# Two transformer blocks in one kernel: other places for some copies, sums and splits in the first attention

## The chip, the cores and the metric

The kernel runs on one core of one Trainium2 chip. The metric is the device time of one execution in microseconds, the median of several. Five engines work side by side, each through its own list of instructions in order: PE (TensorE, matrix products and transposes), DVE (VectorE), ACT (ScalarE), POOL (GpSimd) and SP (SyncE, which here only issues transfers). They meet at semaphores: an instruction waits until a counter has reached a value. An engine that waits holds up all that stands behind in its own list.

## The reference

256 tokens of 1024 numbers go through two blocks, all in float32. The change touches the first block's attention alone:

```python
def rms_norm(x, g):
    xf = x.astype(jnp.float32)
    y = xf * lax.rsqrt(jnp.mean(xf * xf, axis=-1, keepdims=True) + RMS_EPS)
    return (y * g.astype(jnp.float32)).astype(x.dtype)

# diff_attention: 4 heads, each with two maps of 64; moba_attention: 8 heads of 64 (one block of 256 keys)
q = rms_norm(q, q_g); k = rms_norm(k, k_g)          # per head
logits = where(dist >= 0, einsum(q, k) * scale + bias, NEG_INF)
p = softmax(logits)
w = p[:, :, 0] - lam * p[:, :, 1]                    # differential heads only
out = einsum(w, v)
out = rms_norm(out, sub_g) * (1.0 - lambda_init)     # differential heads, per head of 128
...
# first block: x + concat(diff, moba) @ w_out, then x + hier_moe(rms_norm(x))  (32 experts, 2 per token)
# second block: feed forward, window attention and mLSTM, gates, feed forward, final norm
```

## The kernel before, in words

**Precision.** PE multiplies float32 numbers in a faster mode (`float32r`) that keeps fewer digits, so each operand is split into a high part (rounded) and a low part (the rest), and each product is three: high by high, low weight by high, high weight by low (L1072 to L1074).

**Weights.** All dense weights stream through in pieces of 1 MB (128 x 2048 numbers). SP loads a piece into one of three slots (`load`), ACT writes its high part (`split`, L678, 1.9 us), DVE its low part (`split_at`, L1787, 2.3 us), and PE multiplies with it. `feed(q)` on ACT and on DVE splits all pieces up to q + 2 that are not split yet. ACT's split of piece n waits for its transfer and until PE has used piece n - 2 (`piece_used`); the load of piece n waits for DVE's split of piece n - 3 (`split_lo`).

**First attention.** Pieces 0 to 11 are the input projection, two pieces for each of six projections of 512 columns: q and k of the differential heads (projections 0, 1), q and k of the other heads (2, 3), the values of both (4, 5). Tokens come in two halves ("tiles") of 128, t = 0 and 1. For projections 0 to 3:
- ACT squares the result (`qk_squares`, L734), DVE sums per head (`head_squares_of`, L1849), POOL takes the power -1/2 (`root`, L559) and DVE multiplies (`take_projection`, L1867);
- PE transposes the rows (`qk_transpose`, L1143) and ACT copies them out of PSUM into `qkT`, times the gain (`qk_copy(p, t)`, L724).

PE has the scores between its projection products in six bursts (`first_scores`, L1160); DVE adds the bias and takes the maximum (`first_logits`, L1874, L1892), ACT the exponentials (`first_exps`, L739), DVE weighs the two maps (`differential_weights`). Then come, for t = 0 and t = 1, the transposes of the weights on PE (`first_weights`, L1224), their copies by ACT and DVE in turn (`pT_copy`, L709 and L1813), and the products with the values (`first_values(t, units)`, L1253: units 0 to 3 are the differential heads, 128 columns each, and units 4 to 11 the others, 64 columns each). ACT squares the differential heads' output (`heads_squared`, L783), DVE sums it per head, POOL takes the root, DVE multiplies both kinds of heads into `token_major` (`normed_heads`, L1938 to L1946). PE transposes that (`transpose8_tile`, L1089) and ACT and DVE split it into high and low (`t8_split`, L701, L702, L1806, L1807). Last comes the output projection with pieces 12 to 15 (`w_out_part(column half, piece half, t)`), then the router and the expert stage.

**Order.** Nothing is planned by a program: each engine's list stands as written in its block. Queues that matter here: SP's list loads the pieces in turn, waits for 12 used pieces before the gate and up weights of expert 1, for all four value products (`pv` at 4) before those of expert 0, for 16 split pieces before expert 2, and for 16 used pieces before experts 3 and 4. POOL's list has the roots in the order in which DVE asks for them.

## Time and profile before

| | us |
|---|---|
| median of 3 runs | 1100.5 |
| lowest, highest | 1098.31, 1100.85 |
| the profiled execution's own time | 1099.94 |
| its span in the trace | 1098.2 |
| PE busy in it | 1037.1 (94%) |
| DVE, ACT busy | 555.3, 428.0 |

The profile gives for each engine its busy time and, on a timeline, each instruction's start and length, with the idle time before it and who ended that in brackets (short idle times have no bracket). The chain is followed back from the last instruction. Start times are from the start of the span.

### The profile page before, as it was taken

Reading aid. Unit: us, or ns where it says so; the run is one execution under the profiler, and the core shown is the slowest. Engines: PE = TensorE matmul, PEld = TensorE weight load, DVE = VectorE, ACT = ScalarE, POOL = GpSimd, SP = SyncE. Lnnn points to the kernel's source line nnn. Section 1 sums busy time; section 2 is a strip of 40 time slices with the busy share of each in tenths; the row PEclk is TensorE's granted clock in tenths of the full one; section 3 lists DMA queues with packets and bytes.
Section 4 is the critical chain, followed back from the end, with each engine's and each line's share of the span. In section 5 each row is a group of like instructions: output and inputs, shape, how many; then the busy total and the mean of one; then the engine's idle time right before and its main releaser. Section 6 shows DMA issues by size and latency. Waiting matters only on the chain.

```text
span 1098.2 us, 13293 instructions
## 1 busy us (share of the span) xinstructions
PE 1037.1 (94%) x5337; PEld 793.8 (72%) x5337; DVE 555.3 (51%) x844; ACT 428.0 (39%) x564; POOL 48.5 (4%) x57
## 2 busy tenths in 40 slices
PE   7989889999999999999999999978999999999997
PEld 6877777654444458878788899855888888877875
DVE  5477463122222255444546547497656665444443
ACT  4365232322222144343344444384344344444342
POOL 2330000000000000000000000010100010000000
PEclk9999899999999999999999999888999999999999
DMA  8864385999999957555654555411165637555540
GB/s 287 259 228 153 154 349 196 380 418 420 422 421 421 421 170 257 189 185 165 190 187 153 192 177 188 138 54 39 50 239 190 192 115 229 173 191 159 185 153 38
DMA packets 101820, 239.59 MB, mean 218 GB/s; under 512 B 11666, under 2 KB 56810, under 8 KB 86282
## 3 DMA queue, kind: packets, MB, share of 16 engines
q1 hardware_dynamic: 99850, 229.05, 58.0%
q0 software_dynamic: 1920, 9.85, 2.6%
q8 instruction: 34, 0.56, 0.2%
q14 instruction: 16, 0.13, 0.0%
HBM read 237.81 MB, written 3.43 MB: 220 GB/s over the span
## 4 chain that ended last, share of the span: by engine, by line
PE 77%; DVE 8%; issue 5%; ACT 5%; SPq 2%; DMA 2%; POOL 1%; DVEq 0%; ACTq 0%; POOLq 0%
PE banks L1072 17%; PE banks L1074 16%; PE banks L1073 16%; PE banks L1368 8%; PE banks L1393 5%; ACT weights_hi L678 4%; PE banks L1348 3%; PE banks L1377 3%; DMA raw_weights<-in_w_in 2%; DVE stage L2136 1%; DVE weights_lo L1787 1%; PE banks L1079 1%; PE banks L1089 1%; PE banks L1492 1%; SPq L488 1%
## 5 line engine op out<-in xcount | busy, mean ns | idle before, releaser
L1787 DVE TENSOR_TENSOR weights_lo<-raw_weights,weights_hi 128x2048 fp32r<-128x2048 f32 x116 | 265.7, 2291 | 215.4 <-ACT weights_hi L678 215.2
L678 ACT ACTIVATE weights_hi<-raw_weights 128x2048 fp32r<-128x2048 f32 x116 | 221.7, 1912 | 171.7 <-PE banks L1074 154.1
L1072 PE MATMUL banks<-weights_hi,normed_T_hi 128*128 128x512 f32 (+1 forms) x624 | 248.9, 399 | 9.8 <-DVE stage L2136 7.6
L1074 PE MATMUL banks<-weights_hi,normed_T_lo 128*128 128x512 f32 (+1 forms) x624 | 243.4, 390 | 0.0
L1073 PE MATMUL banks<-weights_lo,normed_T_hi 128*128 128x512 f32 (+1 forms) x624 | 242.6, 389 | 0.0
L1072 PEld LDWEIGHTS banks<-weights_hi,normed_T_hi 128*128 128x128 f32 x624 | 118.4, 190 | 42.0 <-DVE stage L2136 13.3
L1074 PEld LDWEIGHTS banks<-weights_hi,normed_T_lo 128*128 128x128 f32 x624 | 118.0, 189 | 25.2
L1073 PEld LDWEIGHTS banks<-weights_lo,normed_T_hi 128*128 128x128 f32 x624 | 118.4, 190 | 22.6
L1072 PE MATMUL banks<-weights_hi,ffn_hidden_T_hi 128*128 128x512 f32 x160 | 62.4, 390 | 0.0
L1074 PE MATMUL banks<-weights_hi,ffn_hidden_T_lo 128*128 128x512 f32 x160 | 62.3, 389 | 0.0
L1073 PE MATMUL banks<-weights_lo,ffn_hidden_T_hi 128*128 128x512 f32 x160 | 62.2, 389 | 0.0
L2064 DVE TENSOR_TENSOR stage<-stage,banks 128x256 f32<-128x256 f32 x16 | 6.7, 422 | 88.7 <-ACT stage L825 88.7
L1368 PE MATMUL banks<-expert_weights,token_major 128*64 128x512 f32 x160 | 49.5, 594 | 0.0
L2056 DVE SCALAR_TENSOR_TENSOR expert_out_lo<-banks,slot_weights,expert_out_hi 128x512 fp32r<-128x512 f32 x32 | 24.0, 750 | 48.2 <-ACT expert_out_hi L831 48.1
L893 ACT ACTIVATE ffn_hidden_T_hi<-banks 128x512 fp32r<-128x512 f32 x20 | 12.0, 598 | 92.3 <-PE banks L1492 92.3
L831 ACT ACTIVATE expert_out_hi<-banks,slot_weights 128x512 fp32r<-128x512 f32 x32 | 22.0, 688 | 61.6 <-PE banks L1393 61.6
L825 ACT ACTIVATE stage<-banks 128x256 f32<-128x256 f32 x16 | 6.2, 386 | 95.7 <-PE banks L1368 71.7
L2160 DVE TENSOR_TENSOR ffn_hidden_T_lo<-banks,ffn_hidden_T_hi 128x512 fp32r<-128x512 f32 x20 | 13.8, 692 | 58.4 <-ACT ffn_hidden_T_hi L893 58.4
L1079 PE MATMUL banks<-ident 128*128 128x128 f32 x244 | 33.7, 298 | 7.8 <-POOL rel_bias L586 7.3
L559 POOL TENSOR_TENSOR rstd<-rstd,minus_half 128x1 f32<-128x1 f32 x12 | 8.6, 721 | 730.5 <-DVE rstd L1753 730.3
L1074 PE MATMUL banks<-normed_T_hi,weights_lo 128*128 128x256 f32 x144 | 40.8, 283 | 0.0
L1073 PE MATMUL banks<-normed_T_lo,weights_hi 128*128 128x256 f32 x144 | 40.8, 283 | 0.0
(358 smaller groups left out, 1664.6 us busy)
## 6 DMA issues: line engine op xcount, KB each, us to landing
raw_weights<-in_w_in SPq DMA_DIRECT2D x38, 1024.0 KB, 5.0
raw_weights<-in_ffn_w_gate SPq DMA_DIRECT2D x44, 512.0 KB, 3.9
raw_weights<-in_ffn_w_up SPq DMA_DIRECT2D x44, 512.0 KB, 4.9
raw_weights<-in_ffn_w_down SPq DMA_DIRECT2D x22, 1024.0 KB, 4.8
stage<-in_w_down SPq DMA_DIRECT2D x14, 1024.0 KB, 12.1
expert_weights<-in_w_gate SPq DMA_DIRECT2D x12, 1024.0 KB, 11.2
expert_weights<-in_w_up SPq DMA_DIRECT2D x12, 1024.0 KB, 13.2
expert_weights<-in_w_down SPq DMA_DIRECT2D x12, 1024.0 KB, 14.3
```

What stands on the lines that cost most here:

```text
L678: ins = eng.activation(w_hi[:, slot, :], raw, ACT.Copy)
L831: eng.activation(exo[0][:, h * HALF:(h + 1) * HALF], PS[:, 7 - h, :], ACT.Copy, scale=wslot[:, 0:1]).then_inc(ex_hi, 1)
L1072: eng.matmul(dst, x[0], w[0], start=first_one, stop=False)
L1073: eng.matmul(dst, x[0], w[1], start=False, stop=False)
L1074: return eng.matmul(dst, x[1], w[0], start=False, stop=last_one)
L1079: eng.matmul(PS[:, bank, 0:P], ident[:, :], ident[:, :], start=True, stop=True)
L1348: mm = eng.matmul(PS[:, 2 * t + h, :], selT[:, u, t * P:(t + 1) * P], exo[x][:, h * HALF:(h + 1) * HALF], start=(first_one and x == 0), st ...
L1368: mm = eng.matmul(PS[SLOTS * m:SLOTS * (m + 1), 6, :], rows[:, k, at + SLOTS * m:at + SLOTS * (m + 1)], gate_up(s)[:, k], start=(k == 0), ...
L1377: mm = eng.matmul(PS[SLOTS * m:SLOTS * (m + 1), 6, cut], rows[:, k, at + SLOTS * m:at + SLOTS * (m + 1)], gate_up(s)[:, k, side], start=(k ...
L1393: mm = eng.matmul(PS[SLOTS * m:SLOTS * (m + 1), 7 - h, :], hidT_e[:, k, SLOTS * m:SLOTS * (m + 1)], down(s)[:, k, h * HALF:(h + 1) * HALF] ...
L1787: ins = eng.tensor_tensor(w_lo[:, slot, :], raw, w_hi[:, slot, :], ALU.subtract)
L2056: eng.scalar_tensor_tensor(exo[1][:, cut], PS[:, 7 - h, :], wslot[:, 0:1], exo[0][:, cut], ALU.mult, ALU.subtract).then_inc(done, 1)
```

## The change

It moves work within four lists and adds or takes away no operation on data.

- **ACT, k rows.** `qk_copy(1, 0)` and `qk_copy(1, 1)` go from behind the split of piece 8 to ahead of the split of piece 7, right behind `qk_copy(0, ...)`.
- **ACT, output.** The split of piece 13 goes ahead of the last exponentials (`first_exps(4, 1, 1)`), the split of piece 14 and the square of half 0's heads ahead of the copies `pT_copy((0, 1))`, the square of half 1's heads ahead of the split of half 0's transposed output.
- **DVE.** `normed_heads` is cut in two. `head_sums` has the reciprocal, the sum per head and the request to POOL; `normed_heads` waits for the root and multiplies. The sums of half 0 go ahead of `pT_copy((0, 1))`, behind the low part of piece 13; the sums of half 1 ahead of the split of half 0; the low part of piece 14 behind both halves.
- **PE.** The transposes of half 0's output stand behind four units of half 1's value products instead of eight; those of half 1 behind one quarter of the output projection instead of two.

```diff
                 if p == 2:
-                    for t in range(TILES):
-                        qk_copy(0, t)
+                    for n in range(2):
+                        for t in range(TILES):
+                            qk_copy(n, t)
                 feed(2 * p + 1)
...
             feed(6)
-            for t in range(TILES):
-                qk_copy(1, t)
             feed(7)
...
             first_exps(3, 0, 1)
+            feed(11, BEFORE_MOE)
             first_exps(4, 1, 1)
             pT_copy((0, 0))
-            pT_copy((0, 1))
-            feed(11, BEFORE_MOE)
+            feed(12, BEFORE_MOE)
...
             heads_squared(0)
-            feed(12, BEFORE_MOE)
+            pT_copy((0, 1))
+            heads_squared(1)
             t8_split(T_Y, yT, vec[:, V_SUB:V_SUB + 1], (0,))
-            heads_squared(1)
...
-            first_values(1, range(8))
+            first_values(1, range(4))
             transpose8_tile(0, tok, (mixed, 2), False)
-            first_values(1, range(8, 12))
+            first_values(1, range(4, 12))
...
             w_out_part(0, 0, 0)
+            transpose8_tile(1, tok, (mixed, 4), False)
             w_out_part(0, 1, 0)
-            transpose8_tile(1, tok, (mixed, 4), False)
...
-            def normed_heads(t):
+            def head_sums(t):
                 eng.wait_ge(expd, EXP_START[t, 1] + MOBA_HEADS)
                 eng.reciprocal(hs[:, t, 5, 8:16], hs[:, t, 2, 8:16])
                 eng.wait_ge(pv_sq, t + 1)
                 link(eng.tensor_reduce(hs[:, t, 7, 0:4], flat(L[t])[:, 0:HALF].rearrange("p (h c) -> p h c", h=4), AX_X, ALU.add))
-                rsqrt(hs[:, t, 7, 4:8], hs[:, t, 7, 0:4], 2 * HEAD)
+                roots[0] += 1
+                eng.tensor_scalar(hs[:, t, 7, 4:8], hs[:, t, 7, 0:4], 1.0 / (2 * HEAD), EPS, ALU.mult, ALU.add).then_inc(root_in, 1)
+                return roots[0]
+
+            def normed_heads(t, root):
+                eng.wait_ge(root_out, root)
...
             take_projection(5)
+            feed(11, BEFORE_MOE)
+            root = head_sums(0)
             pT_copy((0, 1))
-            feed(11, BEFORE_MOE)
-            normed_heads(0)
+            normed_heads(0, root)
+            root = head_sums(1)
+            t8_split(T_Y, yT, vec[:, V_SUB:V_SUB + 1], (0,))
+            normed_heads(1, root)
             feed(12, BEFORE_MOE)
-            t8_split(T_Y, yT, vec[:, V_SUB:V_SUB + 1], (0,))
-            normed_heads(1)
             t8_split(T_Y, yT, vec[:, V_SUB:V_SUB + 1], (1,))
```

The instruction lists show it at three places. First ACT's list around the k rows, before: `weights_hi` is the high part of a piece (7, 8 and 9 here behind 6), L724 the copies of transposed q or k rows.

```order
L678 ACTIVATE weights_hi<-raw_weights 128x2048
L724 ACTIVATE stage<-banks,vec 128x4x128 x2
L678 ACTIVATE weights_hi<-raw_weights 128x2048
L755 ACTIVATE lambda_parts<-lambda_parts 128x2
L757 ACTIVATE router_hi_lo<-router 128x8x36
L759 ACTIVATE w_if_hi<-w_if 128x128
L734 ACTIVATE token_major<-banks 128x512 x2
L678 ACTIVATE weights_hi<-raw_weights 128x2048
L724 ACTIVATE stage<-banks,vec 128x4x128 x2
L678 ACTIVATE weights_hi<-raw_weights 128x2048
```

and with the change:

```order
L678 ACTIVATE weights_hi<-raw_weights 128x2048
L724 ACTIVATE stage<-banks,vec 128x4x128 x4
L678 ACTIVATE weights_hi<-raw_weights 128x2048
L756 ACTIVATE lambda_parts<-lambda_parts 128x2
L758 ACTIVATE router_hi_lo<-router 128x8x36
L760 ACTIVATE w_if_hi<-w_if 128x128
L734 ACTIVATE token_major<-banks 128x512 x2
L678 ACTIVATE weights_hi<-raw_weights 128x2048 x2
```

Two copies left the place between pieces 8 and 9 and stand between pieces 6 and 7.

Second ACT's list from the exponentials of half 0's second group (L739, 128x128) to the split of half 0's output (L701, L702), before:

```order
L739 ACTIVATE conv_room,head_stats<-conv_room,head_stats 128x128 x8
L739 ACTIVATE stage,head_stats<-stage,head_stats 128x256 x8
L709 ACTIVATE conv_room<-banks 128x512
L709 ACTIVATE stage<-banks 128x512 x3
L678 ACTIVATE weights_hi<-raw_weights 128x2048
L783 ACTIVATE conv_room<-banks 128x512
L678 ACTIVATE weights_hi<-raw_weights 128x2048
L701 ACTIVATE mixed_T_hi<-banks,vec 128x4x128
L702 ACTIVATE mixed_T_hi<-banks 128x4x128
L783 ACTIVATE stage<-banks 128x512
```

and with the change:

```order
L739 ACTIVATE conv_room,head_stats<-conv_room,head_stats 128x128 x8
L678 ACTIVATE weights_hi<-raw_weights 128x2048
L739 ACTIVATE stage,head_stats<-stage,head_stats 128x256 x8
L709 ACTIVATE conv_room<-banks 128x512
L678 ACTIVATE weights_hi<-raw_weights 128x2048
L782 ACTIVATE conv_room<-banks 128x512
L709 ACTIVATE stage<-banks 128x512 x3
L782 ACTIVATE stage<-banks 128x512
L701 ACTIVATE mixed_T_hi<-banks,vec 128x4x128
L702 ACTIVATE mixed_T_hi<-banks 128x4x128
```

Both splits (pieces 13 and 14) and both squares (L782) stand earlier; the three copies of half 1 (L709, `stage`) stand later.

Third DVE's list from the values' copy of projection 5 on, before: L1813 copies transposed weights of half 1, L1940 is the sum per head, L1942 and L1946 the two multiplications into `token_major`.

```order
L1862 COPY stage<-banks 128x512 x2
L1813 COPY stage<-banks 128x512 x3
L1787 TENSOR_TENSOR weights_lo<-raw_weights,weights_hi 128x2048
L1938 RECIPROCAL head_stats<-head_stats 128x8
L1940 TENSOR_REDUCE head_stats<-conv_room 128x4
L1747 TENSOR_SCALAR head_stats<-head_stats 128x4
L1942 TENSOR_TENSOR token_major<-banks,head_stats 128x512
L1946 TENSOR_TENSOR token_major<-banks,head_stats 128x512
L1787 TENSOR_TENSOR weights_lo<-raw_weights,weights_hi 128x2048
L1806 SCALAR_TENSOR_TENSOR mixed_T_lo<-banks,vec,mixed_T_hi 128x4x128
L1807 TENSOR_TENSOR mixed_T_lo<-banks,mixed_T_hi 128x4x128
```

and with the change:

```order
L1861 COPY stage<-banks 128x512 x2
L1786 TENSOR_TENSOR weights_lo<-raw_weights,weights_hi 128x2048
L1937 RECIPROCAL head_stats<-head_stats 128x8
L1939 TENSOR_REDUCE head_stats<-conv_room 128x4
L1941 TENSOR_SCALAR head_stats<-head_stats 128x4
L1812 COPY stage<-banks 128x512 x3
L1946 TENSOR_TENSOR token_major<-banks,head_stats 128x512
L1950 TENSOR_TENSOR token_major<-banks,head_stats 128x512
L1937 RECIPROCAL head_stats<-head_stats 128x8
L1939 TENSOR_REDUCE head_stats<-stage 128x4
L1941 TENSOR_SCALAR head_stats<-head_stats 128x4
L1805 SCALAR_TENSOR_TENSOR mixed_T_lo<-banks,vec,mixed_T_hi 128x4x128
```

The low part of piece 13 and the sums of half 0 went ahead of the three copies, and the low part of piece 14 is gone from between the multiplications and the split of half 0.

## Rows read from the trace of the kernel before

**Rows 1.** The page: the chain that ended last, by engine.

```profile
PE 77%; DVE 8%; issue 5%; ACT 5%; SPq 2%; DMA 2%; POOL 1%; DVEq 0%; ACTq 0%; POOLq 0%
```

**Rows 2.** Waits of PE, 40 to 147 us (total, times, longest us).

```profile
PE banks L1089 <- DVE token_major L1946: 3.7, 1, 3.7
PE banks L1160 <- ACT stage L724: 2.8, 1, 2.8
```

**Rows 3.** Timeline of PE, first scores (start, length, idle before in brackets).

```profile
61.93 1.34 PE L1160 MATMUL banks<-stage 64*128 64x128 f32 x16 [2.76 <-ACT stage L724]
...
70.17 1.03 PE L1143 MATMUL banks<-ident,token_major 128*128 128x128 f32 x8
...
78.93 0.66 PE L1143 MATMUL banks<-ident,token_major 128*128 128x128 f32 x4
```

**Rows 4.** Timeline of ACT, k rows to the first exponentials.

```profile
54.42 1.92 ACT L678 ACTIVATE weights_hi<-raw_weights 128x2048 fp32r<-128x2048 f32 x1 [4.15 <-DMA raw_weights<-in_w_in]
...
61.21 1.25 ACT L724 ACTIVATE stage<-banks,vec 128x512 f32<-128x512 f32 x2
...
67.77 0.40 ACT L739 ACTIVATE conv_room<-conv_room,head_stats 128x128 f32<-128x128 f32 x1 [3.52 <-DVE head_stats L1892]
...
71.83 1.91 ACT L678 ACTIVATE weights_hi<-raw_weights 128x2048 fp32r<-128x2048 f32 x1
```

**Rows 5.** Timeline of DVE in the same stretch.

```profile
67.65 2.28 DVE L1787 TENSOR_TENSOR weights_lo<-raw_weights,weights_hi 128x2048 fp32r<-128x2048 f32 x1
72.32 0.43 DVE L1874 CUSTOM_DVE_ANT_0 stage<-banks,stage 128x256 f32<-128x256 f32 x1 [2.39 <-PE banks L1160]
...
75.29 2.28 DVE L1787 TENSOR_TENSOR weights_lo<-raw_weights,weights_hi 128x2048 fp32r<-128x2048 f32 x1
77.49 0.68 DVE L1867 TENSOR_TENSOR token_major<-banks,head_stats 128x512 f32<-128x512 f32 x1
```

**Rows 6.** Timeline of POOL: two roots of projection 2, one of half 0's heads.

```profile
60.72 4.41 POOL L559 TENSOR_TENSOR head_stats<-head_stats,minus_half 128x8 f32<-128x8 f32 x2 [13.14 <-DVE head_stats L1853]
...
114.02 1.01 POOL L559 TENSOR_TENSOR head_stats<-head_stats,minus_half 128x4 f32<-128x4 f32 x1 [34.95 <-DVE head_stats L1747]
```

**Rows 7.** Timeline of PE, value products of half 1 and the transposes.

```profile
108.93 3.79 PE L1253 MATMUL banks<-stage 128*128 128x128 f32 x32 [0.69 <-ACT stage L709]
116.40 1.97 PE L1089 MATMUL banks<-ident,token_major 128*128 128x128 f32 x8 [3.68 <-DVE token_major L1946]
118.16 3.51 PE L1253 MATMUL banks<-stage 128*128 128x64 f32 x16
```

**Rows 8.** Timeline of ACT, last exponentials and the split of piece 13.

```profile
96.42 0.51 ACT L739 ACTIVATE stage<-stage,head_stats 128x256 f32<-128x256 f32 x1 [4.51 <-DVE head_stats L1892]
...
108.78 1.90 ACT L678 ACTIVATE weights_hi<-raw_weights 128x2048 fp32r<-128x2048 f32 x1
```

**Rows 9.** Timeline of DVE, low part of piece 13 to that of piece 14.

```profile
110.71 2.29 DVE L1787 TENSOR_TENSOR weights_lo<-raw_weights,weights_hi 128x2048 fp32r<-128x2048 f32 x1 [2.17 <-ACT weights_hi L678]
...
115.06 0.69 DVE L1942 TENSOR_TENSOR token_major<-banks,head_stats 128x512 f32<-128x512 f32 x1 [1.19 <-POOL head_stats L559]
...
116.26 2.28 DVE L1787 TENSOR_TENSOR weights_lo<-raw_weights,weights_hi 128x2048 fp32r<-128x2048 f32 x1
```

**Rows 10.** Stretches (length, busy us and instructions of PE, PEld, DVE, ACT, POOL; PEclk, DMA share, GB/s).

```profile
114.00:116.00 2.00, 0.00 (x0) 0.00 (x0) 0.94 (x2) 0.00 (x0) 1.01 (x1) 0.50 0.01 4
...
320.00:350.00 30.00, 28.78 (x134) 12.72 (x132) 7.53 (x16) 6.07 (x10) 0.00 (x0) 1.00 1.01 421
```

**Rows 11.** The chain in order of time: output projection (start, us).

```profile
123.92 0.43 PE banks L1074
124.34 0.24 PE banks L1072
```

**Rows 12.** Timeline of PE, second products of two expert pairs in a row.

```profile
355.20 0.61 PE L1393 MATMUL banks<-expert_weights,stage 128*64 128x512 f32 x1 [0.61 <-DVE stage L2066]
...
369.05 0.61 PE L1393 MATMUL banks<-stage 128*64 128x512 f32 x1 [0.61 <-DVE stage L2066]
```

## The prediction

> **What bounds the kernel now.** First the page: 77% of the chain that ended last is PE [rows 1], so a change on ACT or DVE is worth what it takes from PE's waits and from its stretches at half clock. Second the waits of PE in the first attention: two are long, 3.7 us for half 0's output in `token_major` and 2.8 us for copied k rows [rows 2]; the change aims at both. Third the timelines around each, to see what is late next. Fourth the clock: a long wait is followed by products at half pace.
>
> *The k wait.* PE is through projection 3's first piece at 61.93 - 2.76 = 59.2 and stands until ACT's second k copy is out [rows 3]. ACT was not short of time: it idled 4.15 us before piece 7 for that piece's transfer, but had the k copies behind piece 8 [rows 4].
>
> *The output wait.* PE ends eight units of half 1's values at 112.7 and waits until 116.4 [rows 7]. Behind that wait is a row of single steps: ACT splits piece 13 (108.78, [rows 8]), DVE takes its low part (110.71), sums, has the root from POOL (1.01 us, [rows 6]) and multiplies (115.06, then the second product) [rows 9]. In the wait the clock is at 0.50 [rows 10], 1.2 of 2.4 GHz, and it stays there: eight transposes take 1.97 us where eight took 1.03 [rows 3, 7], 16 products of 64 columns 3.51 us where 32 took 3.79 [rows 7], and the wide products start every 0.43 us until 124.34, then every 0.24 [rows 11].
>
> **Part 1, the k rows.** PE's transposes of k stand 24 products before 59.2; at 0.23 to 0.24 us each [rows 11] they end near 53.7. ACT is idle then. The second copy starts there and takes 1.25/2, so both are out at about 54.4, when piece 7 lands (54.42, [rows 4]). Piece 7 is delayed by 0.1 us at most, and nothing behind it waits.
>
> PE then has the first scores at 59.2 to 60.5, projection 3's second piece to 66.1, the transposes of projection 2 to 67.0. What is late next is DVE: the second burst of scores waits until the first burst's maxima are taken, that is until DVE starts piece 9's low part at 67.65 [rows 5]. Nothing moves DVE up to there (its list waited for projection 2's roots on POOL, 60.72 to 65.13, [rows 6]). So PE waits some 0.7 us, has scores to 68.8, products to 74.4, the third burst to 75.5, and needs projection 3's multiplied rows. On DVE those stand behind piece 10's low part. Its high part is made on ACT behind the first exponentials, which start at 67.77 whatever the change does, so at 71.83 + 1.91 = 73.74 [rows 4] as before. Before, DVE came to it only at 75.29, because the second logits waited for PE until 72.32 [rows 5]. Now DVE ends piece 9 at 69.9 and needs 75.29 - 72.32 = 2.97 us for these logits and the sums: 72.9, before 73.74. So piece 10 starts at 73.8, the multiplication 77.49 - 75.29 = 2.20 us later at 76.0, and it ends at 76.7. PE's transposes stood at 78.93 [rows 3]: **2.2 us** earlier. PE stands about 1.2 us there, shorter than either long wait.
>
> From there to the values the rest keeps its distance: PE, whose products run without a long wait, leads; the roots and exponentials have moved by 1.5 us or more with half a microsecond or more to spare. Bounds of this term: 0 (piece 10 keeps its time after all, should POOL's roots delay DVE) and 4.1 (the 2.76 us and 1.3 us of half pace, nothing late next). I take 2.2, the value the rows give.
>
> **Part 2, the output.** All times below are before's less 2.2. ACT's split of piece 13 goes into the idle 4.51 us before the last exponentials [rows 8]: it needs 11 used pieces, which PE gives 2 to 3 us before those exponentials are due, and takes 1.9: hidden. Were it late, the exponentials would be, and through them the transposes of weights, one for one. The split of piece 14 falls in the time in which ACT only waits for transposes and values of half 0.
>
> DVE: the values' copy ends at 101.4, piece 13's low part takes 2.2 (101.3 to 103.6), reciprocal, sum and request 0.9 to 104.5. The first of the three copies of half 1 is ready at about 104.0, so it is 0.4 us late; PE needs its bank again only when it has transposed four banks, near 105.1: hidden, 0.1 at most. Copies end at 106.4; the root, asked at 104.5, takes 1.01 alone and half of 4.41 beside DVE [rows 6], so by 106.7; both multiplications end at 107.6 to 108.0. PE starts half 1's values at 106.8; four units take 3.79/2 = 1.9, to 108.6. So the transposes find their rows, with 0.6 to 1.0 us to spare, and the 3.68 us wait is gone.
>
> What is late next? The split of half 0: transposes to 109.6, ACT 1.2, DVE 1.3, ready at 112.3. PE covers it with eight units, 3.79 us, to 113.3: 1 us to spare. Half 1: squares at 109.3, its root by 111.5 to 112.7, multiplications behind the last values (113.3) to 114.1; PE is in one quarter of the output projection (12 products, 2.8 us) to 116.0. Its split is ready by 120, used at 122.6. Piece 14's low part ends by 116.6, used near 119.8; piece 15 waits for PE as before.
>
> If PE does not stand, the half clock behind the wait goes too. It cost 1.97 - 1.03 = 0.94 (transposes), 3.51 - 3.79/2 = 1.61 (values), and of the 2.8 us of wide products to 124.34 the share 1 - 0.24/0.43, 1.25. **Sum of part 2:** 3.68 + 0.94 + 1.61 + 1.25 = 7.5 us. Bounds: 0 (another step takes the wait's place whole) and 7.5.
>
> **Behind it.** SP issues expert 1's gate and up 2.2 us earlier, expert 0's weights with `pv` 4 about 8 us earlier, experts 2 to 4 with the end of the output projection, as far before it as ever. The expert stage, POOL's list and the second block keep their distances: 0.
>
> **Total.** 2.2 + 7.5 = 9.7 us. The profiled execution took 1099.94 us (span 1098.2), so 1090.2; it lies 0.56 under the median of the runs, and on the median's footing this is 1100.5 - 9.7 = **1090.8**.
>
> **Rival A: the clock falls without a wait.** Half 1's values with 64 columns now stand in one run of 32 products, not 16 + 16, behind eight transposes. Before, the clock fell after 16 such products and part of the wait [rows 7, 10], and 16 of them at half clock did not bring it back; only the wide products did. Against it: up to 112.7 PE had just had 24 transposes and 16 narrow products and ran 32 at 0.118 us each, full pace [rows 7]. If it falls halfway through the run, 16 products cost 1.61 and the wide ones 1.25 again: 1090.8 + 2.9 = 1093.7. A rule bears on it: the Trainium skill (TensorE: Matmul & The Clock Gate, Part 4: PE-mode transpose) has it that transposes on PE don't count as busy for the clock. By that rule the transposes ahead of the narrow run speak for the fall, and the time would be this rival's; the full pace at 108.93, right behind the weights' transposes, doesn't bear it out.
>
> **Rival B: part 1 gives nothing.** DVE and ACT set the pace between 60 and 80 us, and PE only waits elsewhere (at the second burst and the q rows). For it: POOL's roots took 4.41 us for two [rows 6], and a later one holds DVE. Against: the root of the first half is asked at about 72.2 and has 3.8 us. Then 1100.5 - 7.5 = 1093.0.
>
> **Rival C: slower, by the experts' weights.** From 320 to 350 us the queues are full (share 1.01, 421 GB/s) [rows 10], while PE takes a pair every 369.05 - 355.20 = 13.85 us [rows 12]. A pair's six transfers of 1024 KB are 6.3 MB, 14.9 us at that rate: the weights lose 1.1 us on PE with each pair and live on the lead from the loads before. If the shorter attention ate that lead, PE would go at 14.9 for some 12 pairs, 13 us: 1090.8 + 13 = 1103.8. It decides from the point where the lead is 9.7 us too short. Against it: loads 0 and 2 to 4 hang on counters that move with PE, so the lead moves along, and PE shows no wait for a transfer there.
>
> **Rival D: no change.** Both waits come back in another place (ACT's list is tight, or the half clock stays): 1100 to 1101.
>
> **Chances.** Forecast 0.68 (its own range 1089.2 to 1092.4), A 0.15, B 0.12, C 0.02, D 0.03. The range to 8 in 10 takes in A and B's middle: 1088.8 to 1094.0. About 0.3%, 3.3 us, can be told from no change; forecast, A and B lie beyond it: faster 0.95, same 0.03, slower 0.02.
>
> **What would show it.** In the changed kernel's trace: no idle before PE's first scores and their start near 59.2; a wait of under 1 us before the second burst and of about 1 before projection 3's transposes, those near 76.7; the transposes of half 0 near 108.6 without a wait, clock 1.00 to the end of the output projection; its last product 9.7 us earlier than before; every later stretch as long as before. Wrong would be: exponentials pushed behind piece 13, a wait for `mixed_T_lo` before the first quarter, a clock of 0.50 behind the 64-column run, or waits for weights among the experts.

## The result, and the profile after

| | before | changed |
|---|---|---|
| median of the first comparison, us | 1099.7 (15 runs) | 1092.6 (15 runs) |
| lowest, highest | 1096.7, 1102.3 | 1087.6, 1095.9 |
| the profiled execution's own time | 1099.94 | 1090.14 |
| its span | 1098.2 | 1088.3 |
| PE busy in it | 1037.1 | 1031.6 |

The ratio is 0.9932 [0.9918, 0.9946]: 7.1 us between the medians, 9.8 us between the two profiled executions. The forecast was 9.7 us, as a time 1090.8, and the range 1088.8 to 1094.0 holds the median. Two later comparisons of the same kernels gave 0.992 [0.9895, 0.9945] and 0.991 [0.989, 0.9931]. Over all three the mean of 49 executions of before is 1100.6 and that of 27 of the changed kernel 1092.0: 8.6 us (7.6 to 9.6). So the profiled execution of the changed kernel is 1.9 us better than its mean, that of before 0.6 us; why executions of one kernel differ is a question of its own below.

The chain by engine has nearly kept its shape [rows 1]. PE's share has grown from 77 to 79%, and the 4% of SP's queue and of transfers (SPq, DMA) are no longer in it:

```profile
PE 79%; DVE 8%; issue 6%; ACT 6%; POOL 1%; DVEq 0%; ACTq 0%; POOLq 0%
```

Waits of PE from 40 to 147 us, the stretch of [rows 2]. Both long ones are gone:

```profile
PE banks L1142 <- DVE token_major L1866: 1.2, 1, 1.2
PE banks L1088 <- DVE token_major L1758: 1.0, 1, 1.0
PE banks L1159 <- DVE head_stats L1873: 0.9, 1, 0.9
PE banks L1252 <- ACT conv_room L709: 0.8, 1, 0.8
PE banks L1252 <- ACT stage L709: 0.7, 1, 0.7
PE banks L1312 <- DVE routed_T_lo L1803: 0.6, 1, 0.6
```

The first and the third are new, the two short waits that the prediction named as "what is late next". The second and the sixth stand behind the output projection; before has them too, with 1.0 and 0.6 us, but past 147 us. PE's timeline at the first scores, for [rows 3]: the scores start 2.7 us earlier without a wait, projection 3's transposes 2.1 us earlier (76.86, before 78.93).

```profile
59.24 1.16 PE L1159 MATMUL banks<-stage 64*128 64x128 f32 x16
65.92 1.03 PE L1142 MATMUL banks<-ident,token_major 128*128 128x128 f32 x8
...
67.83 1.14 PE L1159 MATMUL banks<-stage 64*128 64x256 f32 x8 [0.88 <-DVE head_stats L1873]
...
76.86 0.66 PE L1142 MATMUL banks<-ident,token_major 128*128 128x128 f32 x4 [1.17 <-DVE token_major L1866]
```

ACT in the same stretch, for [rows 4]: the k rows stand in the idle time before piece 7, and the split of piece 7 starts 0.16 us later than before.

```profile
53.43 1.27 ACT L724 ACTIVATE stage<-banks,vec 128x512 f32<-128x512 f32 x2 [4.46 <-PE banks L1142]
54.58 1.92 ACT L678 ACTIVATE weights_hi<-raw_weights 128x2048 fp32r<-128x2048 f32 x1
```

DVE, for [rows 5]: piece 10's low part now waits for ACT's high part, not for PE.

```profile
67.80 2.28 DVE L1786 TENSOR_TENSOR weights_lo<-raw_weights,weights_hi 128x2048 fp32r<-128x2048 f32 x1
...
73.92 2.29 DVE L1786 TENSOR_TENSOR weights_lo<-raw_weights,weights_hi 128x2048 fp32r<-128x2048 f32 x1 [0.60 <-ACT weights_hi L678]
76.13 0.68 DVE L1866 TENSOR_TENSOR token_major<-banks,head_stats 128x512 f32<-128x512 f32 x1
```

PE in the output, for [rows 7]. Four units, eight transposes and eight units follow each other without a wait and at full pace:

```profile
106.95 2.05 PE L1252 MATMUL banks<-stage 128*128 128x128 f32 x16 [0.69 <-ACT stage L709]
108.84 1.04 PE L1088 MATMUL banks<-ident,token_major 128*128 128x128 f32 x8
109.72 3.68 PE L1252 MATMUL banks<-stage 128*128 128x64 f32 x32
```

ACT, for [rows 8]: piece 13's split stands in the idle time ahead of the last exponentials, and 0.81 us of it is left.

```profile
91.59 1.91 ACT L678 ACTIVATE weights_hi<-raw_weights 128x2048 fp32r<-128x2048 f32 x1 [1.79 <-PE banks L1073]
94.32 0.51 ACT L739 ACTIVATE stage<-stage,head_stats 128x256 f32<-128x256 f32 x1 [0.81 <-DVE head_stats L1891]
```

DVE, for [rows 9]: low part, sums, three copies, two multiplications. The root comes from POOL beside the copies (for [rows 6]), and the rows are ready at 107.8, 1.0 us before PE's transposes.

```profile
101.38 2.28 DVE L1786 TENSOR_TENSOR weights_lo<-raw_weights,weights_hi 128x2048 fp32r<-128x2048 f32 x1
...
103.69 0.63 DVE L1939 TENSOR_REDUCE head_stats<-conv_room 128x4 f32<-128x512 f32 x1
...
106.48 0.68 DVE L1946 TENSOR_TENSOR token_major<-banks,head_stats 128x512 f32<-128x512 f32 x1
107.08 0.68 DVE L1950 TENSOR_TENSOR token_major<-banks,head_stats 128x512 f32<-128x512 f32 x1
```

```profile
104.67 1.01 POOL L559 TENSOR_TENSOR head_stats<-head_stats,minus_half 128x4 f32<-128x4 f32 x1 [26.97 <-DVE head_stats L1941]
```

Stretches, with the columns of [rows 10]. The clock is 1.00 throughout the output, and the transfers among the experts are as before:

```profile
107.00:110.00 3.00, 3.00 (x28) 3.00 (x28) 1.19 (x4) 0.68 (x2) 0.00 (x0) 1.00 0.00 0
110.00:114.00 4.00, 4.00 (x35) 3.87 (x35) 3.04 (x6) 1.09 (x2) 1.01 (x1) 1.00 0.02 4
...
118.00:136.00 18.00, 18.00 (x81) 14.90 (x80) 5.68 (x7) 3.38 (x4) 0.29 (x1) 1.00 0.71 287
320.00:350.00 30.00, 28.78 (x132) 12.55 (x130) 8.30 (x18) 7.33 (x12) 0.00 (x0) 1.00 1.01 420
```

The last product of the first attention, before and then changed (PE's timeline): it starts 9.7 us earlier, and that is the gain of the pair but for 0.2 us (the spans differ by 9.9).

```profile
145.51 0.39 PE L1074 MATMUL banks<-weights_hi,mixed_T_lo 128*128 128x512 f32 x1
```

```profile
135.80 0.39 PE L1073 MATMUL banks<-weights_hi,mixed_T_lo 128*128 128x512 f32 x1
```

### The profile page after: what moved, and what is told of

Read it like the earlier page. It is cut to its first block, busy times and chain, and to the rows that moved or that the text cites. A ratio compares the mean times of both kernels' runs of the same rounds, so it can differ in the third digit from the quotient of the medians.

```text
span 1088.3 us, 13293 instructions
## 1 busy us (share of the span) xinstructions
PE 1031.6 (95%) x5337; PEld 790.1 (73%) x5337; DVE 555.3 (51%) x844; ACT 428.1 (39%) x564; POOL 49.1 (5%) x57
## 4 chain that ended last, share of the span: by engine, by line
PE 79%; DVE 8%; issue 6%; ACT 6%; POOL 1%; DVEq 0%; ACTq 0%; POOLq 0%
PE banks L1071 17%; PE banks L1073 17%; PE banks L1072 17%; PE banks L1367 8%; PE banks L1392 5%; ACT weights_hi L678 4%; PE banks L1347 3%; PE banks L1376 3%; DVE stage L2142 1%; PE banks L1078 1%; DVE weights_lo L1786 1%; PE banks L1088 1%; PE banks L1491 1%; PE banks L1252 1%; PE banks L1223 1%
```

## The experiments

Each kernel was timed beside the kernel before, whose medians were 1099.7 to 1101.4. This table takes the starts of four groups on PE's timeline from each profile; "A" is from half 1's first value product to the last product of the output, "B" from there to the end of the span.

| kernel | scores | projection 3's transposes | half 1's values | last product | A | B | median, us |
|---|---|---|---|---|---|---|---|
| before | 61.93 | 78.93 | 108.93 | 145.51 | 36.6 | 952.7 | 1099.7 to 1101.4 |
| k rows alone | 59.07 | 77.51 | 107.52 | 144.74 | 37.2 | 953.3 | 1099.4 |
| output alone | 62.70 | 79.70 | 109.83 | 138.63 | 28.8 | 953.4 | 1092.7 |
| changed | 59.24 | 76.86 | 106.95 | 135.80 | 28.9 | 952.5 | 1092.6 |
| changed, second | 59.62 | 77.53 | 107.67 | 136.48 | 28.8 | 952.5 | 1091.0 |
| changed, third | 59.68 | 77.30 | 107.44 | 136.28 | 28.8 | 952.8 | 1091.2 |
| wide values | 59.77 | 77.39 | 107.52 | 136.36 | 28.8 | 952.8 | 1092.6 |
| PE's order old | 59.65 | 77.27 | 107.36 | 137.45 | 30.1 | 954.5 | 1092.7 |
| PE's order new, lists old | 59.58 | 77.20 | 107.21 | 146.68 | 39.5 | 952.5 | 1102.4 |
| more idle products | 59.31 | 76.94 | 107.03 | 135.87 | 28.8 | 952.5 | 1090.6 |
| sums late | 61.55 | 79.55 | 109.56 | 139.52 | 30.0 | 952.5 | 1093.8 |
| split late | 59.84 | 77.57 | 107.58 | 136.39 | 28.8 | 956.1 | 1091.7 |
| narrow products mixed in | 59.34 | 76.97 | 107.06 | 135.86 | 28.8 | 952.3 | 1089.6 |

**Part 1 alone.** The first part of the change, on the kernel before:

```diff
-                    for t in range(TILES):
-                        qk_copy(0, t)
+                    for n in range(2):
+                        for t in range(TILES):
+                            qk_copy(n, t)
...
-            for t in range(TILES):
-                qk_copy(1, t)
```

> Part 1 of the change alone: the two k copies ahead of the split of piece 7, all else as before. Theory (the changed kernel's trace): PE's first scores start near 59.2 without a wait, projection 3's transposes near 76.8 instead of 78.93, and the 3.7 us wait at the output stays, 2.1 us earlier: 2.0 to 2.3 us faster than before in the median, about 1097.5. Rival (part 1 carries no gain, what the first parts save comes back at the waits of 0.9 and 1.2 us with a fallen clock): 0 to 0.5 us.

Measured: 1099.43, ratio 0.9988 [0.9971, 1.0005]. As a time that is 0.5 us slower to 3.2 us faster: neither no change nor the expected 2.0 to 2.3 us is ruled out, and the median is 0.7 us under that of before, not 2. In its trace the k wait is gone, but projection 3's transposes come only 1.4 us earlier and the last product 0.8 us. Piece 7 was not there yet when ACT had done the copies:

```profile
55.23 1.92 ACT L678 ACTIVATE weights_hi<-raw_weights 128x2048 fp32r<-128x2048 f32 x1 [0.70 <-DMA raw_weights<-in_w_in]
```

The output wait stands, as long as before and with the same eight transposes at half pace:

```profile
114.99 1.97 PE L1088 MATMUL banks<-ident,token_major 128*128 128x128 f32 x8 [3.68 <-DVE token_major L1945]
```

In before's profile the wide products are back at full pace from 124.1 us, here from 124.0, though the work came 1.4 us earlier. So nine of them, not six, ran at half pace, and A is 0.6 us longer:

```profile
115.00:120.00 5.00, 5.00 (x24) 5.00 (x25) 3.93 (x5) 1.66 (x3) 0.00 (x0) 0.50 0.00 0
120.00:124.00 4.00, 4.00 (x11) 3.14 (x11) 1.67 (x4) 0.00 (x0) 1.01 (x1) 0.50 0.65 227
124.00:130.00 6.00, 6.00 (x31) 5.06 (x30) 0.18 (x1) 1.18 (x2) 0.00 (x0) 0.98 0.95 365
```

**Part 2 alone.** All other edits, k rows where they were.

> Part 2 alone: the new order of splits, sums, squares and transposes at the output, k copies where they were. Theory: the wait of 3.7 us and the half clock behind it go, 7.5 us in an execution whose clock stays up and about 5 in the median, 1094.5, because in some executions the clock falls in or behind the run of 64-column products. Rival (the median's missing 2.6 us belongs to the k part): the full 7.5 us in the median, 1092.2.

Measured: 1092.65, ratio 0.9911 [0.9882, 0.994]. That is the rival's 1092.2, not the theory's 1094.5. A falls by 7.8 us (36.6 to 28.8), and is the same with the k rows moved too. In this profile and in the second of the changed kernel ACT had piece 6 at the same time (47.96 and 48.04); between them the k rows move the last product from 138.63 to 136.48: 2.15 us. The timed runs of the two don't show it: the medians are 1092.65 and 1091.05, the means of six executions each 1091.6 and 1091.9.

**The changed kernel again,** without an edit.

> The changed kernel once more, for a second profile and the spread of its times. Theory (clock): times spread over some 8 us in two groups by mean granted clock, one near 1090 at 0.984 and one near 1093 to 1095 at 0.978 to 0.981, and a profile out of the second group shows a stretch of 0.50 in the first attention that the first profile does not have, behind the 64-column products. Rival (transfers or waits vary): a slow execution shows a longer wait of PE there at full clock.

Measured: 1091.05, ratio 0.992 [0.9895, 0.9945], the same picture, 0.7 us later from the second burst on (68.50 for 67.83).

**Wider value products.** For rival A: 14 of the 16 narrow products of half 1 take 128 columns in place of 64 (the added columns are overwritten by the next unit). The trace has two rows for each of these products, 32 in all; the prediction and the expectations count rows.

```diff
-                            dst, v = PS[:, 2 * t + 1, h * HEAD:(h + 1) * HEAD], vals[:, kb, HALF + h * HEAD:HALF + (h + 1) * HEAD]
+                            n = 2 * HEAD if t == 1 and u < 11 else HEAD
+                            dst, v = PS[:, 2 * t + 1, h * HEAD:h * HEAD + n], vals[:, kb, HALF + h * HEAD:HALF + h * HEAD + n]
```

> The changed kernel with half 1's value products of the second kind of heads made 128 columns wide instead of 64: the upper 64 columns of each are the next head's place and are written anew by the next head's product, so the output stays. Rows of 64 and of 128 columns took the same 0.118 us, so in an execution without a clock fall nothing changes (1090). Theory (the clock falls because of the narrow run): the group of slower executions goes, median 1090 to 1091, 2 us under the changed kernel. Rival (the clock falls elsewhere, at the waits of 0.9 and 1.2 us or later): same spread and median as the changed kernel, 1092.6.

Measured: 1092.61, ratio 0.9926 [0.9898, 0.9954]. Neither the time nor the pace moves: the products take 3.68 us at 64 columns and at 128. Its row of PE's timeline, then its stretch:

```profile
110.28 3.68 PE L1253 MATMUL banks<-stage 128*128 128x128 f32 x32
```

```profile
105.00:120.00 15.00, 14.31 (x103) 12.93 (x102) 10.06 (x16) 4.73 (x8) 2.02 (x2) 1.00 0.35 126
```

**PE's order undone.**

```diff
-            first_values(1, range(4))
+            first_values(1, range(8))
             transpose8_tile(0, tok, (mixed, 2), False)
-            first_values(1, range(4, 12))
+            first_values(1, range(8, 12))
...
             w_out_part(0, 0, 0)
-            transpose8_tile(1, tok, (mixed, 4), False)
             w_out_part(0, 1, 0)
+            transpose8_tile(1, tok, (mixed, 4), False)
```

> The changed kernel, with PE's two new places of half 0's and half 1's transposes undone (eight units of half 1's values ahead of half 0's transposes, two quarters of the output ahead of half 1's), ACT's and DVE's lists as changed. Theory (the lists carry the gain, PE's order is worth the cover of one split): half 0's rows are there near 108.6, so the transposes stand behind 32 narrow products, from 110.7 without a wait, and end at 111.6, 1.9 us later than with the change; their split takes the 2.7 us that it took there (109.7 to 112.4), is ready near 114.3, and PE, through with its values at 113.4, waits 0.9 us at the clock 1.00. Ratio to the changed kernel 1.001, time about 1 us above it and 6 to 7 us below the kernel before. Rival (PE's order carries the gain): the wait of 3 us or more and the half clock come back, 4 us or more above the changed kernel.

Measured: 1092.73, ratio 0.9917 [0.9893, 0.994]; the changed kernel in the same study had 1091.19. The transposes follow without a wait, and the split of half 0 is late by what was expected:

```profile
110.99 1.04 PE L1088 MATMUL banks<-ident,token_major 128*128 128x128 f32 x8
111.87 1.90 PE L1252 MATMUL banks<-stage 128*128 128x64 f32 x16
114.68 0.50 PE L1071 MATMUL banks<-weights_hi,mixed_T_hi 128*128 128x512 f32 x1 [0.91 <-DVE mixed_T_lo L1806]
```

**PE's order alone.** The converse: k rows and PE's order as changed, ACT's and DVE's lists of the output as before.

> The kernel before with the k rows ahead of piece 7 and PE's new order in the output, but ACT's and DVE's lists of the output as before. Theory (lists carry the gain): half 0's rows come where they came, 2.2 us or less earlier than before's 116.4, so near 114.3 to 115; PE is through with four units at 108.7 and waits 5.5 to 6.5 us instead of 3.7; behind it eight transposes and 32 value products at the clock 0.50 (2.0 and 7 us, the second 3.3 more than at full clock). About 3 us slower than the k rows alone: 1100 to 1104, ratio to before 1.000 to 1.004. Rival (PE's order carries the gain): within 2 us of the changed kernel, ratio 0.993 to 0.995.

Measured: 1102.43, ratio 1.0015 [1.0, 1.0031]. The wait is longer by the four units that no longer stand before it, and everything behind it runs at half pace:

```profile
114.67 1.97 PE L1088 MATMUL banks<-ident,token_major 128*128 128x128 f32 x8 [5.41 <-DVE token_major L1945]
```

```profile
115.00:125.00 10.00, 10.00 (x45) 9.61 (x44) 5.37 (x8) 1.66 (x3) 1.01 (x1) 0.50 0.10 16
```

So of part 2's 7.8 us the lists are worth 6.5 to 7.1 without PE's order (A 30.1 against 36.6 of before and 37.2 of the k rows alone), and PE's order is worth 1.3 with them (30.1 to 28.8) and costs 2.3 to 2.9 without them (39.5 against 37.2 of the k rows alone and 36.6 of before).

**The sums late.** One edit of DVE's list undone.

```diff
             feed(11, BEFORE_MOE)
-            root = head_sums(0)
             pT_copy((0, 1))
+            root = head_sums(0)
             normed_heads(0, root)
```

> The changed kernel with one edit undone on DVE alone: the reciprocal, the sums and the root of half 0's heads stand behind the three copies of half 1's weights again, the low part of piece 13 ahead of them as changed. Theory (the gain sits in the row of single steps on DVE; the low part's place is most of it, the sums' place the last microsecond): DVE ends piece 13's low part at 103.7, the copies at 106.1 to 106.3, then reciprocal, sums and request 0.9 to 107.1, the root 1.01 alone to 108.1, the multiplications at 108.1 and 108.8, rows at 109.5; PE is ready at 108.84 and waits 0.6 to 0.9 us, clock 1.00. About 0.7 to 1 us above the changed kernel, ratio to before 0.992 to 0.994. Rival (the sums' place carries the gain): the wait is 3 us or more and the clock falls.

Measured: 1093.77, ratio 0.9934 [0.9914, 0.9955]. The root is a step of the row again (DVE's timeline), and PE waits 0.95 us; A is 1.1 us longer:

```profile
109.86 0.17 DVE L1941 TENSOR_SCALAR head_stats<-head_stats 128x4 f32<-128x4 f32 x1
111.22 0.69 DVE L1946 TENSOR_TENSOR token_major<-banks,head_stats 128x512 f32<-128x512 f32 x1 [1.19 <-POOL head_stats L559]
```

```profile
112.56 1.09 PE L1088 MATMUL banks<-ident,token_major 128*128 128x128 f32 x8 [0.95 <-DVE token_major L1950]
```

In this profile piece 6 also landed late (ACT waited 7.50 us for it to 49.98, in before's profile 5.04 us to 47.20), and all behind it is 1.9 to 2.3 us later than in the third profile of the changed kernel.

**The split late.** The converse: piece 13's split behind the copies on ACT, its low part behind the multiplications on DVE.

```diff
             first_exps(3, 0, 1)
-            feed(11, BEFORE_MOE)
             first_exps(4, 1, 1)
             pT_copy((0, 0))
-            feed(12, BEFORE_MOE)
...
             pT_copy((0, 1))
+            feed(11, BEFORE_MOE)
             heads_squared(1)
             t8_split(T_Y, yT, vec[:, V_SUB:V_SUB + 1], (0,))
+            feed(12, BEFORE_MOE)
...
-            feed(11, BEFORE_MOE)
             root = head_sums(0)
             pT_copy((0, 1))
             normed_heads(0, root)
+            feed(11, BEFORE_MOE)
```

> The changed kernel with the other edits of the lists undone: the split of piece 13 on ACT behind the copies of half 1's weights, its low part on DVE behind half 0's multiplications, the split of piece 14 behind half 0's output, the sums ahead of the copies and PE's order as changed. Theory (what had to go is the low part between the copies and the sums; whether it goes ahead of all or behind all is one to half 0): half 0's rows are there by 107.5, no wait before the transposes; ACT splits piece 13 from 106.8 to 108.7, DVE takes its low part to 111.0, then the low part of half 0 (ACT ready near 111), which ends at 113.0 to 113.5 where PE needs it at 113.0: a wait of 0 to 0.8 us, clock 1.00. 0 to 1 us above the changed kernel. Rival (the split ahead of the exponentials is what frees the output): a wait of 2 us or more before the first quarter or the transposes and a stretch at 0.50 between 105 and 125.

Measured: 1091.69, ratio 0.9916 [0.9887, 0.9945], A 28.8 as in the changed kernel: no wait and full clock. The split ahead of the exponentials was not needed. What had to go was piece 13 from ahead of half 0's sums, and behind the multiplications its low part is as well placed as ahead of everything. Both this run and the one before keep the square of half 0 ahead of the copies on ACT. In the kernel before it stood behind piece 13's split, at 110.58 with 0.59 us, and DVE's sum could not have started before 111.2, only 1.8 us ahead of its 113.03. So by this estimate DVE's low part alone, moved away with ACT's list as it was, would have given about half of the 3.7 us wait; no run tried that.

**More idle products.** The kernel multiplies the identity by itself (`stay_warm`) while PE waits; here it does so more, also before the two new short waits.

```diff
+                            stay_warm(3, 0)
                             first_scores(1)
...
+                            eng.wait_ge(qk_done, 5)
+                            stay_warm(4, 4)
                             qk_transpose(3, 0)
...
-            stay_warm(12, 3)
+            stay_warm(20, 3)
             eng.wait_ge(assigned, 1)
```

> The changed kernel with more products of no use while PE waits: 8 more (16 rows, 1.95 us) before the wait of 2.43 us for the router's assignments, 3 before the second burst of scores (wait of 0.88 us), 4 before projection 3's transposes (wait of 1.17 us). Theory (the clock falls behind such waits, and what differs from one execution to the next is where): the stretch at 0.50 near 155.4 (3 us in the profiles, 1.6 to 1.7 us of PE's time) is gone, the rest of the profile is as in the changed kernel, the profiled execution takes 1088.4 to 1089.5, the median is 1 to 2 us under the changed kernel's. Rival 1 (the clock there falls whatever PE does in that wait): the stretch stays, time as the changed kernel within 0.5 us. Rival 2 (the added products are late and push the assignment's products): 0.3 to 1 us slower.

Measured: 1090.65, ratio 0.9908 [0.9889, 0.9927], the changed kernel beside it 1091.19. My theory of the clock fell. The wait of 2.43 us for the router's assignments is down to 0.65, and the clock falls at 155 all the same (first row); in the third profile of the changed kernel the whole wait is there, and it doesn't (second row):

```profile
155.00:158.00 3.00, 3.00 (x18) 3.00 (x17) 2.62 (x15) 0.00 (x0) 0.00 (x0) 0.57 0.36 147
```

```profile
155.00:158.00 3.00, 3.00 (x28) 3.00 (x28) 2.66 (x14) 0.04 (x1) 0.00 (x0) 1.00 0.51 216
```

**The changed kernel a third time.**

> The changed kernel once more, without an edit, for its executions and one more profile. Theory (the median differs from the profiled pair because the clock falls in other places from one execution to the next): medians between 1090.5 and 1093, executions in two groups by mean clock, 0.984 or more at 1087.5 to 1091 and 0.978 to 0.981 at 1091 to 1096; a profile in the second group shows one or two more stretches at 0.50 than the first ones, and none between 100 and 125 us. Rival (the output's clock is the one that falls in the slower group): such a profile has a clock of 0.50 between 100 and 125 us.

Measured: 1091.19, ratio 0.991 [0.989, 0.9931]; its executions lie at mean clocks of 0.981 to 0.984, and its profile is again one of 0.984.

**Narrow products mixed in.** In the second block 48 products of 16 columns (the gates) stand in one run, behind 14 us in which PE has no idle time and a clock of 1.00; in their course the clock falls, in the profiles of all the kernels above. The changed kernel, stretches before and across:

```profile
662.00:676.00 14.00, 14.00 (x80) 12.27 (x79) 13.00 (x23) 7.81 (x12) 0.00 (x0) 1.00 0.56 187
...
680.00:684.00 4.00, 4.00 (x23) 3.90 (x23) 1.64 (x4) 2.22 (x2) 0.00 (x0) 0.62 0.80 262
684.00:688.00 4.00, 4.00 (x12) 3.09 (x11) 3.23 (x5) 0.00 (x0) 0.00 (x0) 0.53 0.24 55
```

The experiment puts three of them behind each of the 16 triples of the projection piece ahead:

```diff
                                 mm = product(z_bank(n)[:, 0:HALF - lo], ...)
+                            if g == 6:
+                                gate = units_of[9][narrow // KT]
+                                j, i2 = narrow % KT, Z[gate][2]
+                                nn = product(z_bank(gate)[:, 0:16], both(hT, lambda h: h[:, j, i2 * P:(i2 + 1) * P]),
+                                             both(w_if_parts, lambda w: w[:, j, :]), j == 0, j == KT - 1)
...
+                                narrow += 1
```

> The changed kernel with the 48 products of 16 columns for the gates (676.9 to 683.4 in its profile) no longer in one run, but three of them behind each of the 16 triples of 512 columns of the projection piece ahead of them. Same products, same weights. Theory (it is a run of such narrow products, and not a wait, that takes the clock down near 681; PE has no idle time in the 20 us before): the stretch at 0.50 of 6 to 10 us near there goes, PE gets back 3.4 to 5 us, the profile shows 1.00 from 662 to 707, the median lies 3 to 5 us under the changed kernel's: 1087 to 1089, ratio to before 0.987 to 0.990. Rival 1 (the clock falls there for another reason): it falls in the same place and the time is the changed kernel's. Rival 2 (it falls a little later, in the second attention, where PE waits): half the gain.

Measured: 1089.64, ratio 0.9909 [0.9875, 0.9942]. The clock stays:

```profile
680.00:684.00 4.00, 4.00 (x23) 3.45 (x22) 1.40 (x3) 1.87 (x2) 0.00 (x0) 1.00 0.79 262
684.00:688.00 4.00, 4.00 (x19) 3.32 (x18) 3.50 (x5) 0.47 (x1) 0.00 (x0) 1.00 0.08 12
```

PE comes to the second attention's scores 2.84 us earlier (705.95 for 708.79) and leaves that attention 0.16 us earlier (769.10 for 769.26). In between it doesn't wait more (idle for 10.6 us, the changed kernel for 11.1), but the clock is lower, 0.80 in place of 0.86 from 720 to 770; the rows of this kernel and then of the changed one:

```profile
720.00:770.00 50.00, 42.95 (x264) 33.23 (x265) 36.40 (x115) 20.58 (x58) 1.67 (x1) 0.80 0.07 22
```

```profile
720.00:770.00 50.00, 41.78 (x279) 32.81 (x278) 38.99 (x131) 23.33 (x71) 1.67 (x1) 0.86 0.07 22
```

Of the expected 3 us or more 2.8 were earned, and 2.7 of them given back at the lower clock. That is the second rival, which had put half the gain as lost. No kernel tried here beats the changed one by more than these runs can tell.

## Why the prediction was right

**Part 1, the k rows (2.2 us).** Right in mechanism and, in the traces, in size, with one bound that the prediction underrated; in the timed runs the term by itself is not told from nothing. Scores at 59.24 without a wait (forecast 59.2), a wait of 0.88 before the second burst (0.7), 1.17 before projection 3's transposes (1.2), these at 76.86 (76.7), piece 10's low part at 73.92 (73.8). The term is 2.1 us in the pair and 2.15 in the second one (output alone against changed). But with the k rows ahead nothing is left on ACT to hide a late piece 7: where its split started 0.65 us later than in the changed kernel (55.23 for 54.58), the transposes did too, and the term was 1.4 us (k rows alone). The prediction counted the delay of piece 7 by the copies, not its landing.

**Part 2, the output (7.5 us).** Right: 9.7 less part 1's 2.1 is 7.6 in the pair, and A says 7.7 to 7.8, which is 0.2 to 0.3 above the sum and its upper bound. That the total met 9.7 to a tenth owes something to luck: part 1 was put 0.1 too high, part 2 a little too low. The steps, before's times less 2.2 and the trace: half 0's rows ready at 107.6 to 108.0, trace 107.8; transposes at 108.6, trace 108.84; split of half 0 ready at 112.3, trace 112.5 (111.79 + 0.68); values through at 113.3, trace 113.4. The half clock behind the wait (3.8 of the 7.5) went with the wait. What the prediction had no view of is which edit carries it. The two experiments on the lists show that piece 13 may go out of the row of steps in either direction, and that the sums' place is worth 1.1 us; the places of ACT's squares and of half 1's steps were not tried by themselves.

**Rival A, the narrow run.** Wrong here: 32 rows of 64 columns behind eight transposes take 3.68 us at a clock of 1.00 in every profile with PE's new order and the changed lists, and widening them changes nothing. The Trainium skill (TensorE: Matmul & The Clock Gate, Part 4: PE-mode transpose) has it that transposes don't count as busy in the same way as products and that the full clock doesn't engage for them. The traces don't bear it out here: 24 + 8 transposes from 103 to 110 us ran at 1.00. The thought that the clock can fall in a narrow run without a wait was not wrong: it does in the run of 16 columns (680 to 688 us above).

**Rivals B, C and D.** B fell with projection 3's transposes: POOL had the first of their roots at 74.3, and DVE took it at 76.13. C: PE shows no wait for a transfer among the experts, its wait for DVE there is 9.7 us in 16 times before and after, the transfers move 420 GB/s as before. D: no wait came back.

**Behind it, 0.** B in the table is 952.7 before and 952.5 changed; it goes up to 956.1 in other profiles, by the clock (next paragraph).

**The median.** The sum was made for one pair of profiled executions and set on a median of three runs. The pair gave 9.8, the means over 49 and 27 executions 8.6 (7.6 to 9.6). The missing microsecond is not in the output: in all three profiles of the changed kernel A is 28.8 to 28.9 at full clock. Some of it is ahead of the output: the second and third profile have the last product at 136.48 and 136.28, 0.7 and 0.5 us behind the first (135.80), and 0.4 us of that is there at 36 us already, ahead of all that was changed (ACT's split of the piece before piece 6 starts at 36.20 and 36.26, in the first profile at 35.83). Two things are seen to move an execution by some microseconds in places that no edit touched. One is where the clock falls later on. In the profile of the split late, B is 956.1, not 952.5, and its router stretch is at half clock for longer than the changed kernel's:

```profile
153.00:156.00 3.00, 2.60 (x13) 2.60 (x13) 1.74 (x7) 0.00 (x0) 0.00 (x0) 0.51 0.98 412
156.00:160.00 4.00, 4.00 (x20) 4.00 (x21) 3.10 (x16) 0.00 (x0) 0.00 (x0) 0.52 0.14 59
```

The stretch of the 16-column products varies too. From 147 to 165 us the mean clock is 0.91 in the first profile of the changed kernel, 1.00 in the third and 0.81 in that of the split late; from 676 to 692 us it is 0.79, 0.68 and 0.69. A difference in mean clock times the length of the stretch gives an estimate of the time: the third profile gained 1.6 us in one place and lost 1.8 in the other, and its B is 952.8; the split late lost 1.8 and 1.6, 3.4 of the 3.6 us in its B.

The changed kernel's executions go by the clock too: the 11 with a mean clock of 0.984 take 1090.7 on average, the 5 with 0.978 take 1095.0. The other is when the first pieces land: piece 7 0.8 us later with the k rows alone than in before's profile, and piece 6 in the sums late so much later that all behind it is 1.9 to 2.3 us late. All three profiles of the changed kernel had a clock of 0.984, so where it falls in its slower executions was not seen in that kernel itself, and stays open; nor is it shown why its profiled ones are better than its mean.

## What to carry to other kernels

When an engine waits at the end of a row of single steps, look for the long independent instructions that stand in the row (here a split of 1.9 us on one engine and its low part of 2.3 us on the next) and move them out, forward or back; ask for a root before the copies, not behind them. Reordering the waiting engine alone made things worse by 2.3 to 2.9 us, and was worth 1.3 once the row was short: mend what it waits for first. A wait costs more than its length where the clock falls behind it: here 3.7 us of wait and 3.8 us of half pace.

## What of the hardware was not expected

- Products of 64 and of 128 columns cost the same: 32 rows take 3.68 us in both.
- In a run of 48 products of 16 columns, without any idle time of PE, the granted clock fell from 1.00 to 0.50 in every profile that has the run; in the one profile with the same 48 mixed with products of 512 columns it did not. The run of 32 rows of 64 columns kept 1.00.
- The same kernel has a clock of 0.55 from 155 to 158 us in one execution and 1.00 in another, with the same waits before it; in a third profile 1.8 us of the 2.4 us wait there were filled, and the clock was 0.57.
- Two roots of 128x8 on POOL took 5.03 us (1.64 and 3.32), the second while DVE had a low part from 73.92 to 76.2; before, two took 4.41 [rows 6]. One root of 128x4 took 1.01 beside copies. No run tells the share of the size from that of DVE's work.
